# A trunk kernel's memory probabilities: block turns on VectorE and a trip through DRAM in place of TensorE transposes

## What is computed

```python
def memory_attention(q, mem_k, mem_v):
    ...
    s = jnp.einsum('bthd,bmhd->bhtm', qh, kh).astype(jnp.float32) * (MEM_HEAD_DIM ** -0.5)
    p = jax.nn.softmax(s, axis=-1).astype(vh.dtype)
    o = jnp.einsum('bhtm,bmhd->bthd', p, vh)
    return o.reshape(b, t, D_MEM)

def layer_a(...):
    ...
    y_mem = memory_attention(q_mem, mem_k, mem_v) * jax.nn.silu(g_mem)
    return h + jnp.concatenate([y_rnn, y_mem], axis=-1) @ w_out
```

## Time and profile before

| | |
|---|---|
| median of three runs | 1468.18 us |
| profiled execution: its span, first to last instruction | 1466.5 us |
| TensorE busy | 1458.0 us, 99% of the span |
| VectorE, ScalarE, GpSimd busy | 997.5, 716.3, 122.8 us |
| 16 DMA engines, mean rate | 244 GB/s |

### The profile page before, as it was taken

One profiled execution on the slowest core, in us unless ns is written; L12 is line 12 of the kernel. 1 busy time (PEld: TensorE's weight loads), 2 busy tenths in 40 slices (PEclk: granted clock), 3 DMA queues, 4 the chain that ended last, 5 costly groups with the idle time before them and its releaser, 6 DMA issues.

```text
span 1466.5 us, 18207 instructions
## 1 busy us (share of the span) xinstructions
PE 1458.0 (99%) x6842; PEld 1221.7 (83%) x6842; DVE 997.5 (68%) x1317; ACT 716.3 (49%) x1066; POOL 122.8 (8%) x184
## 2 busy tenths in 40 slices
PE   9999999999999999999999999999999999999998
PEld 7888888888888888888888888888888888888886
DVE  6775568465576896856579676556566566578987
ACT  6764544444544645763325654433333433455465
POOL 0001111111110000000010001111111011000000
PEclk9999999999999999999999999999999999999999
DMA  9877788777886987477989876687888888858853
GB/s 344 290 287 225 159 215 228 174 235 158 212 251 165 323 323 260 155 262 282 358 326 372 291 224 219 244 218 196 230 241 244 202 239 208 226 188 329 315 200 144
DMA packets 154189, 357.97 MB, mean 244 GB/s; under 512 B 7824, under 2 KB 23440, under 8 KB 150032
## 3 DMA queue, kind: packets, MB, share of 16 engines
q1 hardware_dynamic: 103824, 205.98, 40.3%
q0 software_dynamic: 29376, 102.77, 28.3%
q10 hardware_dynamic: 20928, 48.41, 9.0%
HBM read 310.99 MB, written 113.25 MB: 289 GB/s over the span
## 4 chain that ended last, share of the span: by engine, by line
PE 99%; DMA 0%; SPq 0%; ACT 0%; issue 0%; DVE 0%; ACTq 0%
PE main L2128 25%; PE main L2127 25%; PE main L2126 25%; PE aux L2127 6%; PE aux L2126 6%; PE aux L2128 6%; PE aux L2484 2%; PE aux L2473 1%; DMA w_raw<-in_w_mem_kv 0%; PE aux L2270 0%; PE main L2178 0%; PE aux L2178 0%; PE main L2199 0%; PE main L2202 0%; PE main L2205 0%; PE aux L2220 0%
## 5 line engine op out<-in xcount | busy, mean ns | idle before, releaser
L2126 PE MATMUL main<-act_hi,w_hi 128*128 128x512 f32 x1216 | 475.3, 391 | 0.0
L2127 PE MATMUL main<-act_lo,w_hi 128*128 128x512 f32 x1216 | 473.6, 389 | 0.0
L2128 PE MATMUL main<-act_hi,w_lo 128*128 128x512 f32 x1216 | 473.6, 389 | 0.0
L2128 PEld LDWEIGHTS main<-act_hi,w_lo 128*128 128x128 f32 x1216 | 228.3, 188 | 47.4
L2127 PEld LDWEIGHTS main<-act_lo,w_hi 128*128 128x128 f32 x1216 | 228.4, 188 | 46.7
L2126 PEld LDWEIGHTS main<-act_hi,w_hi 128*128 128x128 f32 x1216 | 228.4, 188 | 46.4
L1334 DVE SCALAR_TENSOR_TENSOR w_lo<-w_raw,gains,w_hi 128x512 fp32r<-128x512 f32 x180 | 123.3, 746 | 120.5 <-ACT w_hi L704 120.5
L704 ACT ACTIVATE w_hi<-w_raw,gains 128x512 fp32r<-128x512 f32 x180 | 115.4, 712 | 140.6 <-PE main L2128 121.9
L1325 DVE TENSOR_TENSOR w_lo<-w_raw,w_hi 128x1024 fp32r<-128x1024 f32 x88 | 104.1, 1222 | 105.2 <-ACT w_hi L697 105.0
L697 ACT ACTIVATE w_hi<-w_raw 128x1024 fp32r<-128x1024 f32 x88 | 88.5, 1057 | 169.5 <-PE main L2128 132.7
L2126 PE MATMUL main<-w_hi,act_hi 128*128 128x512 f32 (+1 forms) x432 | 163.5, 378 | 0.0
(11 more groups left out here) (321 smaller groups left out, 1861.4 us busy)
## 6 DMA issues: line engine op xcount, KB each, us to landing
w_raw<-in_w_in_a SPq DMA_DIRECT2D x32, 1024.0 KB, 6.7
w_raw<-in_w_in_b SPq DMA_DIRECT2D x32, 1024.0 KB, 7.9
weight_sums<-in_w_out_a POOLq DMA_DIRECT2D x48, 512.0 KB, 7.0
weight_sums<-in_w_out_b POOLq DMA_DIRECT2D x48, 512.0 KB, 7.2
weight_sums<-weight_sums POOLq DMA_DIRECT2D x32, 512.0 KB, 6.4
w_raw<-weight_sums SPq DMA_DIRECT2D x16, 1024.0 KB, 6.6
work<-weight_sums SPq DMA_DIRECT2D x16, 1024.0 KB, 7.5
w_raw<-in_w_mem_kv SPq DMA_DIRECT2D x13, 1024.0 KB, 5.2
```

Of the source, the lines that this page charges most:

```text
L2126: TE.matmul(o, a[0], b[0], start=first, stop=False)
L2127: TE.matmul(o, a[0], b[1], start=False, stop=False)
L2128: return TE.matmul(o, a[1], b[0], start=False, stop=final)
```

## The change

For each head, DVE turns the normalised probabilities in blocks of 32x32 from `pm` to `pm_turned` (one instruction). ACT's queue stores the result to a DRAM scratch `prob_scratch` (512 KB, rows of 4 KB), waits for the store, and loads it back with four DMAs of 128 KB (32 partitions each, runs of 1 KB) into the tile that later holds `pmt_lo`. Store and loads together move the four blocks of a 128x128 tile to their places. ACT then copies to `pmt_hi` and DVE subtracts in place, as before, but from SBUF instead of PSUM. The 8 transposes on PE are gone, and the values read their moving operand in runs of 32 elements (`probs_back`). The values of head 3 stand at the end of half u = 0, 12 matmuls later than before. The four semaphores of POOL's weight sums become one counter, and POOL waits for all of group n-1 before it begins group n.

```diff
+    prob_dram = nc.dram_tensor("prob_scratch", [4, 32, 4, 256], F32, kind="Internal").ap()
...
+        pm_turned = work[:, 1024:2048]
+        pmt_at = [w[:].rearrange("p m t -> p (m t)") for w in (pmt_hi, pmt_lo)]
+
+        def probs_back(w, m):
+
+            return w.rearrange("p (r t m j) -> p m t r j", r=4, t=NT, m=NMB)[:, m]
...
+                if n:
+                    pool.wait_ge(sums_made, 16 * 32 * n)
...
+            def probs_store(L, n):
+                act.wait_ge(pt_turned, 4 * L + n + 1)
+                act.dma_start(prob_dram.rearrange("r i c m -> (r i) (c m)"), pm_turned).then_inc(turn_stored, 16)
+
+            def probs_load(L, n):
+                act.wait_ge(turn_stored, 16 * (PROB_TURN[L] + n) + 16)
+                if n:
+                    act.wait_ge(mo_done, 4 * L + n)
+                for c in range(4):
+                    act.dma_start(pmt_at[1][32 * c:32 * c + 32, :].rearrange("p (r m) -> p r m", r=4).bitcast(F32),
+                                  prob_dram[:, :, c, :].rearrange("r i m -> i r m")).then_inc(turn_loaded, 16)
+
             def mem_probs_out(L, n):
-                act.wait_ge(pt_done, 4 * L + n + 1)
+                act.wait_ge(turn_loaded, 64 * (PROB_TURN[L] + n) + 64)
...
                         mem_head(L, j + 1)
+                    probs_store(L, j)
...
                         y_quad(q_k1[0], 1)
+                    probs_load(L, j)
...
                 last.then_inc(p_ready, 1)
+                dve.wait_ge(p_ready, 4 * L + n + 1)
+                V.transpose(pm_turned.rearrange("p (c n j) -> p n c j", c=4, j=32),
+                            pm.rearrange("p t (m c i) -> p (t m) c i", m=NMB, i=32)).then_inc(pt_turned, 1)
...
-                    hooks = {(1 if j == 0 else 0): lambda: mem_scores(L, j), 3: lambda: mem_transposed(L, j)}
+                    hooks = {(1 if j == 0 else 0): lambda: mem_scores(L, j)}
...
-                half(s, 0, m01, 0, 0, values)
-                half(s, 1, m01, 0, 1)
+                half(s, 0, m01, 0, 0, freed(0))
+                half(s, 1, m01, 0, 1, values)
```

More of the change, by code:

```diff
@@ L63 @@
 WT_WIDTH = (512, 512, 256)
+PROB_TURN = (0, 4)
 Z_ORDER = ((1, 3, 0), (0, 2, 384), (2, 2, 0), (3, 1, 0))
@@ L405, in trunk @@
         p_ready = sem("p_ready")
-        pt_done = sem("pt_done")
+        pt_turned = sem("pt_turned")
+        turn_stored = sem("turn_stored")
+        turn_loaded = sem("turn_loaded")
         pt_hi = sem("pt_hi")
@@ L430, in trunk @@
         q22_loaded = [sem(f"q22_loaded{n}") for n in range(2)]
-        sums_made = [sem(f"sums_made{n}") for n in range(4)]
+        sums_made = sem("sums_made")
         sum_ready = sem("sum_ready")
@@ L550, in load_out @@
                 load_quad(y, q_22[s][0], KQ, 4, HALF, q22_loaded[0])
-                sp.wait_ge(sums_made[2 * s], 16 * 32)
+                sp.wait_ge(sums_made, 16 * 32 * (2 * s + 1))
                 load_proj(s, 2)
@@ L562, in load_out @@
                     load_proj(s, u)
-                sp.wait_ge(sums_made[2 * s + 1], 16 * 32)
+                sp.wait_ge(sums_made, 16 * 32 * (2 * s + 2))
                 for u in range(14, N_PROJ):
@@ L616, in _, with move @@
                                     pattern=[[-1, P]], channel_multiplier=1).then_inc(const_ready, 1)
-            def move(n, dst, src, op):
+            def move(dst, src, op):
                 for r in range(4):
                     rows = slice(2 * P * r, 2 * P * r + 2 * P)
-                    pool.dma_start(dst[rows], src[rows], accum_op=op).then_inc(sums_made[n], 16)
+                    pool.dma_start(dst[rows], src[rows], accum_op=op).then_inc(sums_made, 16)
             def store_ht(c):
@@ L666, in _ @@
                         store_value(m)
[L667 to L679, removed]
+                if n:
+                    pool.wait_ge(sums_made, 16 * 32 * n)
+                move(t1, b11, ALU.bypass)
+                move(t3, b12, ALU.bypass)
+                pool.wait_ge(sums_made, 16 * (32 * n + 8))
+                move(t1, b12, ALU.add)
+                move(t3, b22, ALU.add)
+                pool.wait_ge(sums_made, 16 * (32 * n + 16))
+                move(t2, t1, ALU.bypass)
+                pool.wait_ge(sums_made, 16 * (32 * n + 20))
+                move(t2, b22, ALU.add)
+                pool.wait_ge(sums_made, 16 * (32 * n + 24))
+                move(t4, t2, ALU.bypass)
+                pool.wait_ge(sums_made, 16 * (32 * n + 28))
+                move(t4, b21, ALU.add)
         @blk.scalar
@@ L839, in mem_scores @@
                 last.then_inc(p_exp, 1)
+            def probs_store(L, n):
[8 more added lines that the diff above has]
+                                  prob_dram[:, :, c, :].rearrange("r i m -> i r m")).then_inc(turn_loaded, 16)
             def mem_probs_out(L, n):
-                act.wait_ge(pt_done, 4 * L + n + 1)
+                act.wait_ge(turn_loaded, 64 * (PROB_TURN[L] + n) + 64)
                 for m in range(NMB):
-                    nc.scalar.activation(pmt_hi[:, m, :], aux[:, 2 + m, :], ACT.Copy).then_inc(pt_hi, 1)
+                    part = slice(T * m, T * m + T)
+                    nc.scalar.activation(pmt_at[0][:, part], pmt_at[1][:, part].bitcast(F32), ACT.Copy).then_inc(pt_hi, 1)
             def mem_head(L, n):
@@ L1530, in mem_probs_out @@
                     dve.wait_ge(pt_hi, 2 * (4 * L + n) + m + 1)
-                    V.tensor_tensor(pmt_lo[:, m, :], aux[:, 2 + m, :], pmt_hi[:, m, :].bitcast(F32), ALU.subtract
-                                    ).then_inc(pt_lo, 1)
+                    part = slice(T * m, T * m + T)
+                    V.tensor_tensor(pmt_at[1][:, part], pmt_at[1][:, part].bitcast(F32),
+                                    pmt_at[0][:, part].bitcast(F32), ALU.subtract).then_inc(pt_lo, 1)
             def mem_head(L, n):
@@ L2262, in mem_scores, with mem_values @@
                 last.then_inc(ms_done, 1)
-            def mem_transposed(L, n):
-                pe.wait_ge(p_ready, 4 * L + n + 1)
+            def mem_values(L, n):
+                pe.wait_ge(mkv_lo, 4 * L + n + 1)
+                pe.wait_ge(pt_lo, 2 * (4 * L + n) + 2)
                 if n:
@@ L2268, in mem_transposed @@
                 for m in range(NMB):
[L2269 to L2276, removed]
                     last = three_passes(aux[:, 2, :], (mv_hi[:, n % 2, m, :], mv_lo[:, n % 2, m, :]),
-                                        (pmt_hi[:, m, :], pmt_lo[:, m, :]), m == 0, m == NMB - 1)
+                                        [probs_back(w, m) for w in pmt_at], m == 0, m == NMB - 1)
                 last.then_inc(mo_done, 1)
@@ L2318, in values @@
                 def values(t):
-                    freed(0)(t)
-                    if t == 1:
+                    if t == 0:
                         mem_values(s, 3)
```

## The result

Four runs of the changed kernel gave a median of 1513.02 us (1506.99 to 1515.71) beside 1468.68 for the kernel before on the same chip: 1.0297 times the time before, 95% interval 1.0275 to 1.0318, so 44 us slower. Forecast were 1483.8 us and a range up to 1500. The sign was right, the size was not.

What follows compares the result with a forecast made beforehand. PE bounds the kernel, busy 1458.0 of 1466.5 us. Per layer 4.2 + 1.0 + 0 + 6.1 - 3.5 = 7.8 us, two layers +15.6: span 1482.1, median 1483.8 us, range 1474 to 1500.

Steps and rivals of the forecast that it cites:

- the room: Slack before PE waits, read from timelines: 0.65 us at head 0's values, 0.2 us at half u = 2.
- the 7.0: PE's 64 transposes removed: 0.88 us a head, 3.5 us a layer, 7.0 us gained in all.
- S: Store's time from issue to landing on ACT's queue: 5, 4, 3.5, 3 us for heads 0 to 3; bounds 3.0 and 5.6.
- R: Last load's issue to landing: 4.5, 3.5, 3, 3 us for heads 0 to 3; bounds 2.2 and 4.9.
- S - 0.8: PE's wait at the values of head 0, from the store's landing time: 4.2 us forecast.
- Rival (b): DMA crowded everywhere, store 5.6 and load landing 4.9 us: 17.6 us a layer, 1503 us; chance 0.15.
- The round: Heads 1 and 2: ACT's cycle from split to split, 10.2 + S plus R over 3.0, against PE's 13.7 us.
- break-even of 3.5: Store landing time in us from which heads 1 and 2 each begin to cost PE a wait.
- Rival (e): PE's clock falls to 1.2 GHz after waits of 4 to 6 us: some +11 us, 1495; chance 0.07.
- the chain: Head 3: gapless 12.0 us from copies' end to half u = 2's first weights; copies delayed 5.5 us.
- 6.1: PE's wait in us per layer from head 3, at half u = 2, partly already at the values and u = 1.
- what would show it: Profile signs: head 0 waits some 4 us, largest wait at u = 2, copies 5.5 us later, steps over 0.23 us mean clock.

Runs made afterwards that it cites:

- the kernel without a trip: The changed kernel without the DRAM store and loads: ACT copies straight from the turned tile, DVE subtracts from it; 1465.51 us, 0.9978 of before.
- The clock experiment: The kernel before, with ACT doing slab 2's split copy five times over ahead of the split, once per layer, no transfer changed; 1491.95 us.
- the quiet one-hop kernel: The changed kernel with four direct SBUF-to-SBUF DMAs replacing store and loads, and SP's and POOL's transfers held back; 1482.14 us.
- the version with three hops: Against the kernel before: heads 0 to 2 by direct SBUF-to-SBUF DMAs, keys reordered, some transfers held, head 0's values later; head 3 keeps transposes; 1466.85 us.

## Why the prediction failed in its size

**What bounds the kernel, and the direction.** Right: the room was 0.2 to 0.7 us at head 0 and at half u = 2, every wait counted in full, and the transposes were worth nearly what was worked out (the kernel without a trip wins 3.0 us net of 3.0 us of waits at half u = 2, so 6.0 of the 7.0).

**S and R at heads 0 and 1: the step that failed.** "I take S = 5, 4, 3.5, 3" with 5.6 as the upper bound. Measured from the store to the loads: 9.0, 9.3, 2.9 and 3.4 us in layer 0, and 10.2, 5.6, 5.0 and 3.4 in layer 1 (of the two 3.4, part is the wait for `y_quad`). The bound was half of the 11.3 us that a 1 MB store took the earlier trace rows. But a landing behind a backlog is not a price per byte that could be halved: in the trace before, 4.7 of the 11.3 us passed before that store's first packet, while 1.00 MB of SP's and POOL's queues moved. The right reading was in the rows shown: DMA share 1.04 at 329 GB/s where the store would be issued, and a 1 MB load that landed 12.4 us after its issue. A DMA issued there has to be expected to land late though it is small; at head 0 of layer 0 512 KB, in one DMA or in four, took some 9 us in every kernel that left the rings full. With S = 9 the prediction's own formula, S - 0.8, gives 8.2 for head 0 of layer 0, against 8.7 measured. In layer 1 it gives 9.4 against 12.0, because R failed too: from the last load's issue to landing passed 7.3 us, where 4.5 was taken and 4.9 was the bound (6.2 at head 1 of layer 0, with 3.5 taken). Rival (b), "crowded everywhere", asked the right question and was priced with the same bounds.

**Heads 1 and 2.** The round was right in form. Head 1 paid 5.5 us in layer 0 with S = 9.3 and R = 6.2 (forecast 1.0 with S = 4 and R = 3.5); the slower matmuls behind head 0's wait had made PE's own round longer by some 2.5 us. Head 2 paid nothing with S = 2.9, below the break-even of 3.5, and 1.1 us in layer 1 with S = 5.0.

**Rival (e), the clock, was given 0.07, stood at nothing in the sum, and took 11 us.** It was priced at "some +11" and set against the forecast as an alternative, when it came on top of the waits. That 11 came out is chance: it was priced for two stretches of 24 slow matmuls in a layer, half of them hidden, and measured were three of 7 to 12. Behind each of the changed kernel's six waits of 2.3 us and more 7 to 12 matmuls stepped 0.43 us. The clock experiment shows it without the trip. The Trainium skill ("TensorE: Matmul & The Clock Gate", Part 1) has a clock that is low by default and that activity lifts. The trace agrees: 0.51 in the 4 us behind head 0's wait, then 1.00. The length of a wait alone does not tell the price: in the quiet one-hop kernel no matmul stepped 0.43 us behind the 2.5 us at head 0, and seven did behind the 2.0 us at half u = 2.

**Head 3: the chain was right, the delay too large.** From the end of the copies to the first weights of half u = 2 the prediction had 12.0 us; to PE's first matmul with them it was 11.8 (495.81 to 507.60). But the copies came 3.7 us later against DVE's normalisation than before, not 5.5:

```profile
486.97 0.34 ACTq L856 DMA_DIRECT2D prob_scratch<-work  x1
490.34 1.06 ACT L774 ACTIVATE act_hi<-f_raw 128x1024 fp32r<-128x1024 f32 x1 [6.07 <-DVE f_raw L1416]
490.40 1.28 ACTq L863 DMA_DIRECT2D pmt_lo<-prob_scratch  x3
494.66 1.15 ACT L870 ACTIVATE pmt_hi<-pmt_lo 128x512 fp32r<-128x512 f32 x2 [2.30 <-DMA pmt_lo<-prob_scratch]
...
507.60 0.77 PE L2158 MATMUL main<-w_hi,act_hi 128*128 128x512 f32 x1 [3.45 <-DVE w_lo L1400]
```

The loads stand behind `y_quad` in the order, yet they are issued 0.06 us after it begins, not when it ends: the two activations, 2.0 us together, cover the four issues. These 1.8 us (5.5 less 3.7) are most of the 2.6 by which 6.1 was too much.

**The rest.** The turn took 1.25 us (forecast 1.2). The operand in runs of 32 stepped 0.237 us on average where no wait disturbs it (layer 0 of the kernel without a trip), against 0.227 before: 0.06 us a head, near the forecast of nothing. POOL's new waits and the move of head 3's values cost nothing, as the kernel with these parts alone shows. Of the list "what would show it" the places and the causes held, and so did the sign that it gave for the clock. The sizes did not: head 0 waited 8.7 and 12.0 us instead of some 4, head 3's copies came 3.7 us later instead of 5.5, and PE's largest wait was at head 0, not at half u = 2.

## What to carry to other kernels

A transfer put on the critical path costs the backlog in front of it and beside it, and not only its own bytes: before pricing it, read which transfers are under way at its issue and how late the last of them landed, and take such a landing whole, without scaling it by size. That the order is by issue fits these traces; how the engines choose among the queues was not tested. Emptying the rings for it moves the debt to the transfers that wait, so look where those are needed. A wait of TensorE of several us should be priced with the slower matmuls behind it, about 2.4 us for one of 9.

## What the runs showed of the hardware

- ACT's queue issues DMAs while an activation before them still runs (loads at 490.40 during the activation of 490.34).
- The four loads from DRAM mostly took 1.8 us to issue, the four DMAs of a hop 2.5. At head 0 of layer 0 the hop took 3.4 to 4.5 us in all four kernels that have it, also where the DMA engines had moved nothing for 4 us before it (4.15 us in the version with three hops): full rings are not the reason, and what is stays open.
- A store of 512 KB had no packet moved for 4 us while another queue's bytes, issued before it, went out at 334 GB/s.
- DVE's turn of 128x1024 in blocks of 32x32 takes 1.25 us with runs of 32 elements, and 2.02 with elements 4 apart.
- One DMA can spread 32 partitions of 4 KB over 128 partitions of 1 KB, SBUF to SBUF, without DRAM.
